# Layer B's q and k projections of heads 1 to 7, as seven products on token and contraction halves instead of eight

## What is computed

```python
proj = h @ w_in                      # h: 1056 x 1024; q, k, v of one head: 128 columns each
xpad = concatenate([prefix, qkv])    # 3 earlier tokens in front
conv = xpad[:, 0:T] * conv_w[0]
for wi in range(1, CONV_W):          # CONV_W = 4
    conv = conv + xpad[:, wi:wi + T] * conv_w[wi]
q, k, v = split(silu(conv))          # q and k are then normalised
o, S = gated_delta(q, k, v, g, beta, S0)   # chunks: a triangular solve, then a recurrence over chunks
```

## Time and profile before

| | us |
|---|---|
| three runs | 2195.5, 2200.28, 2202.48 (median 2200.28) |
| the profiled execution | 2194.7 |
| its span in the profile | 2192.7 |

### The profile page before, as it was taken

How to read it: one execution, slowest core, us unless ns; L and a number is a source line. 1 busy time by engine, 2 the same in 40 slices (tenths; PEclk the granted TensorE clock), 3 DMA queues, 4 the chain that set the end, 5 groups by cost and what they waited for, 6 DMA issues and landing times.

```text
span 2192.7 us, 46735 instructions
## 1 busy us (share of the span) xinstructions
PE 2154.7 (98%) x19630; PEld 1531.5 (70%) x19630; DVE 938.3 (43%) x2431; ACT 663.8 (30%) x1589; POOL 456.4 (21%) x642
## 2 busy tenths in 40 slices
PE   8999999999999999999999999999999999999998
PEld 6888888888888876544567667676676666665444
DVE  5234354354344444321355555555555233333252
ACT  4122321312222131311234434444344344442101
POOL 0522241242123205000032322322322110020000
PEclk9999999999999999999999999999999999999999
DMA  7412211212221166666012212122110173114451
GB/s 227 154 42 64 81 30 41 78 43 67 58 59 42 35 212 227 213 207 212 13 62 93 70 74 83 67 79 80 60 53 14 40 273 97 39 59 148 136 168 53
DMA packets 210278, 210.99 MB, mean 96 GB/s; under 512 B 14262, under 2 KB 181654, under 8 KB 209151
## 3 DMA queue, kind: packets, MB, share of 16 engines
q1 hardware_dynamic: 198070, 148.27, 22.4%
q0 software_dynamic: 12000, 59.73, 7.1%
HBM read 179.56 MB, written 68.23 MB: 113 GB/s over the span
## 4 chain that ended last, share of the span: by engine, by line
PE 50%; DVE 0%; ACT 0%; issue 0%; POOL 0%; DVEq 0%
PE bank L2088 19%; PE bank L2802 8%; PE bank L3292 7%; PE bank L2146 4%; PE bank L2162 4%; PE bank L2144 2%; PE bank L2154 1%; PE bank L2818 1%; PE bank L2827 1%; PE bank L3270 1%; PE bank L3303 0%; PE bank L2177 0%; PE bank L3199 0%; PE bank L3176 0%; PE bank L2810 0%; PE bank L3186 0%
## 5 line engine op out<-in xcount | busy, mean ns | idle before, releaser
L884 PE MATMUL bank<-arena 128*128 128x256 f32 (+1 forms) x2688 | 631.7, 386 | 0.0
L884 PEld LDWEIGHTS bank<-arena 128*128 128x128 f32 x2688 | 494.5, 190 | 75.3
L2088 PE MATMUL bank<-arena 128*128 128x352 f32 x1296 | 469.2, 474 | 0.1
L2088 PEld LDWEIGHTS bank<-arena 128*128 128x128 f32 x1296 | 214.0, 190 | 58.1 <-ACT arena L2309 0.6
L2802 PE MATMUL bank<-arena 128*128 128x352 f32 x576 | 176.4, 459 | 0.0
L3292 PE MATMUL bank<-arena 128*128 128x512 f32 x360 | 167.5, 599 | 0.0
L2146 PEld LDWEIGHTS bank<-arena 128*128 128x128 f32 x864 | 125.5, 192 | 36.7 <-issue 0.3
L2802 PEld LDWEIGHTS bank<-arena 128*128 128x128 f32 x576 | 106.6, 190 | 53.3
L2162 PEld LDWEIGHTS bank<-arena 32*32 32x32 f32 x7680 | 78.8, 105 | 91.6 <-issue 39.8
L1338 POOL TENSOR_TENSOR arena<-arena 128x272 f32<-128x272 f32 (+1 forms) x48 | 31.5, 656 | 507.6 <-ACT arena L1058 487.6
L2146 PE MATMUL bank<-arena 128*128 128x128 f32 x864 | 131.3, 278 | 0.2 <-ACT arena L2329 0.2
(11 more groups left out here) (426 smaller groups left out, 2720.2 us busy)
## 6 DMA issues: line engine op xcount, KB each, us to landing
arena<-in_w_in_a SPq DMA_DIRECT2D x48, 512.0 KB, 5.1
arena<-in_w_in_b SPq DMA_DIRECT2D x40, 512.0 KB, 4.1
arena<-in_cache_win_k SPq DMA_DIRECT2D x48, 256.0 KB, 5.1
arena<-in_cache_win_v SPq DMA_DIRECT2D x48, 256.0 KB, 3.6
out<-arena SPq DMA_DIRECT2D x40, 256.0 KB, 3.3
arena<-in_w_mem_kv SPq DMA_DIRECT2D x16, 512.0 KB, 8.0
arena<-in_cache_mem_k SPq DMA_DIRECT2D x32, 256.0 KB, 4.1
arena<-in_cache_mem_v SPq DMA_DIRECT2D x32, 256.0 KB, 3.4
```

The source lines that it names most:

```text
L884: m = nc.tensor.matmul(o[:, 0:hi - lo], w, y, start=k == 0 and i in (0, 1, 3, 5), stop=k == KH - 1, skip_group_check=i in (2, 4, 6))
L2088: m = nc.tensor.matmul(bank[j % 3][:, 0:PART], ring.slots[:, (B1 + b) % RING, k, :], part_in(k, part_), start=k == 0, stop=k == KD - 1)
```

## The change

For each head 1 to 7, q is `left` and k is `right`. Tokens are cut in two halves of 528 (a task each), a half in two quarters of 264 columns, the contraction in two halves of 4 blocks. A task t is seven products of 4 units of 264 columns (28 units), where before q and k took 48 units of 352 per head. v stays as three pieces of 8 units. Four weight sums (POOL, 4 x 128 columns each) are made per head, four token sums (POOL, 4 x 264 columns each) per task, and one further subtraction of 264 columns. ACT makes four copies and DVE four additions per task in place of the copies of pieces. Per two groups a head now has 80 units: slots 0 to 7 of a group take three, slots 8 to 15 two (before: slots 0 to 3 three, the others two). In POOL's program the former items stand at fixed slots, and the sums between them, behind the slot in which product 4 or product 6 ends. `product` below is PE's, the other functions are POOL's.

```diff
+    units = plain(0, range(NPB))
+    for h in range(1, HB):
+        units += seven(task_of(h, 0)) + plain(h, (0, 1)) + seven(task_of(h, 1)) + plain(h, (2,))
+    units += plain(HB, range(IN_B))
+    AHEAD = 34
...
+    slots = [[(1, 2)] * 8 + [(1, 1)] * 8] * (NG_ - 3) + [[(1, 2)] * 2 + [(0, 1)] * 12 + [(0, 0)] * 2]
...
+        def product(t, i, k):
...
+                elif i == 2:
+                    pe.wait_ge(tpa, 4 * t + 1)
+                    pe.wait_ge(tws, 4 * (h - 1) + 2)
+                    pe.wait_ge(ttk, 4 * t + 2)
...
+            o, w, y = ((a_of(t), left[:, k, :], hT[:, k, lo:mid]),
+                       (bank[1], left[:, KH + k, :], hT[:, KH + k, lo:mid]),
+                       (a_of(t), ws2[:, k, :], tk2[:, k, :]),
+                       (c_of(t), ws4[:, k, :], hT[:, KH + k, mid:hi]),
+                       (a_of(t), right[:, k, :], tk3[:, k, :]),
+                       (bank[1], right[:, KH + k, :], tk4[:, k, :]),
+                       (a_of(t), ws1[:, k, :], tk1[:, k, :]))[i]
...
+        def weight_sums(h, ns):
...
+                if n == 0:
+                    ring.wait(pool, B1 + 3 * h)
+                    ring.wait(pool, B1 + 3 * h + 1)
+                    v = right[:, 0:KH, :], left[:, 0:KH, :], right[:, 0:KH, :], ALU.subtract
...
+        def token_sums(t, ns):
+            lo, mid, hi = HALVES[t % 2]
+            b11, b12, b21, b22 = (hT[:, k:k + KH, c:c + QUART] for k in (0, KH) for c in (lo, mid))
+            for n in ns:
+                after(pool, tpd, NPROD * (t - 1) + (5, 3, 6, 7)[n])
+                after(pool, ttk, 4 * t + n)
+                v = ((tk3, b22, b12, ALU.subtract), (tk2, tk3, b11, ALU.add), (tk4, b21, tk2, ALU.subtract),
+                     (tk1, b12, b11, ALU.subtract))[n]
+                nc.gpsimd.tensor_tensor(*v).then_inc(ttk, 1)
...
+            for kind, t, i in ended(us):
+                if kind == "product" and i == 4:
+                    pool.wait_ge(tpv, 4 * t + 2)
+                    pool.wait_ge(tpa, 4 * t + 3)
+                    nc.gpsimd.tensor_tensor(s1w, s1w, u3b, ALU.subtract).then_inc(tpp, 1)
+                    if t + 1 < task_of(HB, 0):
+                        token_sums(t + 1, (0, 1))
+                        if t % 2:
+                            weight_sums(2 + t // 2, range(3))
+                elif kind == "product" and i == 6 and t + 1 < task_of(HB, 0):
+                    token_sums(t + 1, (2, 3))
+                    if t % 2:
+                        weight_sums(2 + t // 2, (3,))
...
         nc.gpsimd.memset(xpad[:, :, 0:CW - 1], 0.0).then_inc(xzero, 1)
+        token_sums(0, range(4))
+        weight_sums(1, range(4))
...
+        beside(units[PER_HEAD:PER_HEAD + AHEAD])
         for G in range(NG_ + 1):
...
+            for s in SLOTS:
+                if more and s in SAMPLES_AT:
+                    samples((G + 1) // 2, SAMPLES_AT[s])
+                if s == 1 and G < NUM_EARLY:
+                    copy_part(pool, G)
+                if s == AT_SCALE and G > 1:
+                    scale_outputs(G - 2)
+                if s == AT_SQUARES and G + 2 < NG_:
+                    squares(G + 2)
+                if s == AT_SPREAD and G < NG_:
+                    spread_diagonals(G)
+                beside(units_at(G, s))
```

More of the change, by code:

```diff
@@ L1937, in build @@
     NPB = 9
+    NVB = 3
+    NPR = NPB + NVB * (HB - 1)
+    QUART = TOK // 4
+    HALVES = ((0, QUART, 2 * QUART), (2 * QUART, 3 * QUART, 4 * QUART))
+    tk2, tk3, tk4 = (sb[:, MQ[0] + TOK * n:MQ[0] + TOK * (n + 1)].rearrange("p (k c) -> p k c", c=QUART)
+                     for n in range(3))
+    tk1 = brT[:, 6, :].rearrange("p (k c) -> p k c", c=QUART)
+    s1w = sb[:, MQ[0] + 3 * TOK:MQ[0] + 3 * TOK + QUART]
+    u2b, u3b = brT[:, 11, 768:768 + QUART], brT[:, 7, 0:QUART]
+    ws2, ws4, ws1 = (brT[:, b, c:c + KH * P].rearrange("p (k c) -> p k c", c=P)
+                     for b, c in ((7, 2 * QUART), (9, 256), (10, 0)))
+    tpd, tpa, tpv, tpp, tws, ttk = (sem(f"q_{n}") for n in (
+        "product_done", "product_read_act", "product_read_dve", "third_less", "weight_sums", "token_sums"))
+    a_of = lambda t: bank[2 * (t % 2)]
+    c_of = lambda t: bank[2 - 2 * (t % 2)]
+    first_reads = lambda h, part_: NPB + NVB * (h - 1) + part_ + 1
+    task_of = lambda h, half: 2 * (h - 1) + half
     NWB = 5
@@ L2078, in _, with unit, piece @@
     def _(pe):
[L2079 to L2081 removed]
+        def unit(kind, n, i, k):
+            product(n, i, k) if kind == "product" else piece(n, i, k)
+        def piece(h, j, k):
+            if h == HB:
+                i, part_ = j // 3, j % 3
+            elif h:
+                i, part_ = 2, j
+            else:
+                i, part_ = PIECES[j]
             b = 3 * h + i
+            o = bank[j % 3]
+            if 0 < h < HB:
+                t = task_of(h, int(part_ == 2))
+                o = bank[1] if part_ else c_of(t)
             if k == 0:
@@ L2396, in _ @@
         silu(0, 2)
[L2397 to L2400, removed]
+        silu(1, 0)
+        product(0, 0)
+        silu(1, 1)
+        product(0, 2)
+        silu(1, 2)
+        beside(units[PER_HEAD + 3 * KH:PER_HEAD + AHEAD])
         for G in range(NG_ + 1):
@@ L2721, in spread_diagonals @@
             x.then_inc(spread, 1)
+        def weight_sums(h, ns):
+            left, right = (ring.slots[:, (B1 + 3 * h + x) % RING, :, :] for x in range(2))
+            done = NPROD * (task_of(h, 0) - 1)
+            for n in ns:
[3 more added lines that the diff above has]
+                    v = right[:, 0:KH, :], left[:, 0:KH, :], right[:, 0:KH, :], ALU.subtract
+                elif n == 1:
+                    after(pool, tpd, done + 3)
+                    v = ws2, right[:, KH:KD, :], right[:, 0:KH, :], ALU.subtract
+                elif n == 2:
+                    after(pool, tpd, done + 4)
+                    v = ws4, left[:, KH:KD, :], ws2, ALU.subtract
+                else:
+                    after(pool, tpd, done + 7)
+                    v = ws1, ws2, left[:, 0:KH, :], ALU.add
+                after(pool, tws, 4 * (h - 1) + n)
+                nc.gpsimd.tensor_tensor(*v).then_inc(tws, 1)
```

185 lines of the change are left out of this document (149 added, 36 removed).

## The result

| | before | after |
|---|---|---|
| median of the runs on this chip, us | 2198.66 (2195.5 to 2202.48) | 2333.36 (2331.56 to 2335.49) |
| the profiled execution, us | 2194.7 | 2333.61 |
| granted TensorE clock, mean over the span | 0.997 | 0.966 |

The ratio is 1.061, 95% interval 1.059 to 1.063. The profiled executions differ by 138.9 us.

A forecast was written before the change was run, and what follows sets the result against it. PE, busy 98% of the span, was taken as the bound. Terms of -24.9, +105.6, +9, +8.5 and +29 gave +127 us on 2194.7, so 2322, stated as 2325 for the median; range 2262 to 2365, about 8 in 10.

The forecast's parts named there:

- PE's programme: q and k of seven heads in the loop: cheaper product units on PE, 24.9 us less, the whole gain.
- POOL's prices: POOL's added work: weight sums 1.41 us each, token sums 2.44 or 2.07, subtraction 0.67; POOL about 170 us busier.
- DVE and ACT at nothing: Loop's quarter copies and additions replacing piece copies: costed at nothing, at most 11 us if each addition came late.
- Even groups: Ahead of slot 14: POOL's sums make the spread 10.1 us late, PE loses 9.9 us in each of six groups.
- Odd groups: Ahead of slot 14: spread 6.2 us late, with convolutions holding POOL up PE loses 7.7 us in each of six groups.
- After the even groups: Sums right behind the spread meet convolutions and next group's reads: 1.5 us a group, in all 9 us.
- The beginning: Before head 0's norms: weight sums wait for ring block 4 and delay the squares, costing PE 8.5 us.
- The clock: PE's waits in the loop and beginning bring its clock to half: 13 times 2.2 us, 29 us.
- Hidden: Rival: POOL's sums before the spread delay nothing, leaving PE's shorter programme and the beginning, 2184 us; chance 8%.
- Only even groups: Rival: POOL is early enough in odd groups, so only even groups wait ahead of slot 14, 2266 us; chance 10%.
- Without the clock's fall: Rival: PE waits in the loop but its clock stays up, 2296 us; a fifth of the forecast's own chance.
- convoy: Rival: every loop convolution under a POOL sum delays its slot, and half clock lasts longer, 2367 us; chance 9%.

The follow-up runs named there:

- experiment 6: Kernel of experiment 5 with each of the loop's sums made over one column only, q and k unusable; 2180.34 us, ratio 0.993 to the kernel before.
- experiment 4: Kernel after, with the twelve cache copies that POOL starts in the loop moved to the later block; 2360.4 us, ratio 1.074.
- experiment 1: Kernel after, with each weight and token sum of the loop covering one column, order and waits unchanged; 2274.09 us, ratio 1.035.
- experiment 2: Kernel after, with sums due in slots 8 to 12 held back in POOL's queue until after the spread; 2255.22 us, ratio 1.026.
- experiment 5: Kernel after, only POOL's order changed: sums held past the spread, squares, samples and weight sums moved; 2206.86 us, ratio 1.005.
- experiments 7 to 9: Loop's cache copies in 8 KB runs, in kernel after, in experiment 5, and there with sums and third sample later; 2389.79, 2259.98, 2269.38 us.

## Why the prediction was right

It said slower, 2325 us with 2262 to 2365; the runs gave 2333.4. The way in which the time is lost was forecast, the size of its terms in part by luck. By its own steps:

**PE's programme** (-24.9): right; experiment 6 shows it by itself. **POOL's prices**: right. The 56 token sums took 2.27 us in the mean (forecast 2.07 and 2.44), and POOL has 171.7 us more (forecast 170). **DVE and ACT at nothing**: right but for one copy of ACT's, 3.2 us at the beginning.

**Even groups** (59.4, measured 80.1): the mechanism and the steady value were right (9.9 each; 9.9 to 10.4 from group 4 on). The term is mis-sized by 20.7 us because a step is missing: the prediction priced the weight sums and left out that they wait for a load, though it had named that load for the beginning. Its 3.7 us were from a stretch without the copies; in the loop the k block lands only when the copy of the same group is over, after 28.6 us in the first group and 16 to 20 in the others. Without copies the six waits are 56.3 us (experiment 4), so the late loads cost 24. The trace of before could have told: a load that it issued at 1168.5, 3 us after a copy, took 39.6 us. Nobody waited for it there. The late k block is also why shorter sums alone don't help (experiment 1).

**Odd groups** (46.2, measured 37.8): 6.3 each in place of 7.7. From product 4's end to the spread's POOL took 15.1 us in group 5, where 14.6 were counted and 2.0 added for convolutions that hold it up: of those only 0.5 came. Two slips stand in the working. 6.2 late less 0.24 is 6.0 and not 5.7, and the convolution of the earlier trace rows ended 0.55 us after POOL's instruction and not 0.75.

**After the even groups** (9, none seen): the collisions are there, without their price. The convolution right behind group 4's wait took 1.65 us under a sum (at 1386.29; L2579 takes 0.75 in the mean where the sums are short, experiment 6), but no wait of PE above 0.5 us followed.

**The beginning** (8.5, measured 12.1): 7.7 for the norms, where 8.5 were counted; 3.2 at product 2 of the first task is ACT's copy of a bank (L2421), which was not in the sum and costs in every version.

**The clock** (29, measured 35.3): 14 stretches at half clock more than before, 2.5 us each, where 13 of 2.2 were counted. The long wait of the first group cost no more than the others, for most of its stretch at half clock lay within the wait.

**The rivals.** "Hidden" asked for under 4.4 us of POOL's work between product 4 and the spread; experiment 2 takes the sums out from there and shows that this isn't enough, since they then cost at slot 2, and experiment 5 that even in a good order they cost what the products gain. "Only even groups" fell: both wait. "Without the clock's fall" fell: the clock fell in each of the twelve waits ahead of slot 14. The "convoy" is real but not in this kernel's order. The misses of three terms (+20.7, -8.4 and -9) nearly cancel, so the total is better than its parts, and that is luck. So is a part of the last step: 2322 for the profiled execution and 5.6 more for the median are 2327.5 and not 2325.

## What to carry to other kernels

Work taken off the bound engine and handed to an idle one is paid by what stands behind it in that engine's queue: list what it delays, and by how much, before asking how busy the engine is. For each instruction that is moved or added, ask which load it waits for, and take that load's time from a stretch with the same traffic: here it was set by what was left of the copy at its issue. When a wait has two causes in a row, take away both before judging either.

## What the runs showed of the hardware

- Four DVE products of 1.17 us together took 6.56 us beside POOL sums of 1.4 to 2.3 us, one sum for each (experiment 2).
- A 512 KB load took 3.8 us without the copies (experiment 4). Issued during a 2 MB copy in packets of 65,024 bytes (2.4 us each), the six k blocks of the kernel after took 15.9 to 28.6 us and landed 1.2 to 1.4 us after the copy. With packets of 8 KB (0.31 us each) loads took 24 to 25 us in the median. In both, one packet of the load went through after each packet of the copy.
- Copies in packets of 8 KB held POOL for 48 to 55 us, twice in a run, until the copy before had landed (experiments 7 to 9).
- The granted clock fell to 0.50 1.9 us into a wait of PE of 10.1 us and stayed there for 5.5 us of work behind it; over the loop waits cost a quarter more than they last (35.3 on 131.7 us).
